# Attention by pairs of heads and blocks of queries in a two-block layer kernel

## The chip, the cores and the metric

The kernel runs on one core of a Trainium2 chip. The metric is the time of one launch on the device in microseconds; every figure of a run is that time, and the profiled execution also gives a span, from the first to the last instruction of the program.

## The reference

A sequence of 512 tokens of width 1024 goes through two layers, in float32. The first is a half feed-forward block (SwiGLU, 2816 wide), an attention block, a second half feed-forward block and a norm; the second is a mixing block (convolution and a recurrence) and a feed-forward block. The change lies in the attention block of the first. It has sixteen heads of two kinds, concatenated and projected:

```
# heads 0 to 7: own chunk of 64 and the 8 before it = all keys up to the chunk's end
sc = q_blk @ k.T * 64 ** -0.5 + bias[clip(i - j)]      # q, k, v: 512 x 64
# heads 8 to 15: q, k = 64 columns without and 32 with rotation, the same mask
sc = (q_nope @ k_nope.T + q_pe @ k_pe.T) * 96 ** -0.5
p = softmax(where(key_chunk <= query_chunk, sc, -1e30))
o = p @ v
x = x + concat(out_a, out_b) @ w_out
```

## The kernel before, in words

Activations lie feature by token in SBUF, 128 features to a tile. Weights come as 264 slabs of 128 x 1024, loaded by SyncE's queue into a ring of four (line 318). GpSimd splits each into a high and a low part (`split`, line 332: one pass with one input at line 335, one with two at line 337), and TensorE multiplies with three passes of products (lines 350 to 352). The engines run side by side and meet in semaphores; each works through its own list in order, so the order in which a function is called on an engine is part of the design.

Attention stands between the projections of the block (`in1`, `uq`, `ukv`) and its output projection (`out1`, line 664). It is cut into 64 steps: head h = 0 to 15, and for each head four blocks q of 128 queries, where block q sees L = 128 (q + 1) keys. Heads 2j and 2j+1 lie in the lower and the upper 64 partitions of the same tiles (`qa`, `ka`, or `qn`, `kn`). A step s is:

- TensorE, `scores` (line 597): for heads 0 to 7 one product with 64 rows; for the others one with 64 rows, one with 32 for the rotated part, and one with a single row that writes the mask, all added in one bank. Three banks alternate. In float32 each product is two records of weight load and product.
- VectorE, `score_max` (line 1578): the row maximum; for heads 0 to 7 it also adds the bias (from `relb`) and writes the sums to `prob`.
- ScalarE, `softmax` (line 1098): the exponential with its row sum into `prob`, which has three buffers.
- VectorE, `normalise` (line 1598): reciprocal and multiplication of `prob`.
- TensorE, `turn` (line 621): q + 1 transposes into one of two banks (3, 4).
- ScalarE, `keep_turned` (line 1110): the copy of the turned block to `probT`.

Once a head's four blocks are turned, `values` (line 630) does four products of 128 rows and 64 columns, over 512, 384, 256 and 128 queries, into bank 5 or 6, where the two heads of a pair fill the two column halves. Then `out_hi` on ScalarE (line 1119) and `out_lo` on VectorE (line 1605) split the pair's output for the projection.

TensorE runs one step of scores ahead, and turns two steps behind (lines 641 to 652). Between the steps of the first heads it also spreads the norms of the second kind of heads (`late_norm`, line 581, one in two steps up to s = 27): ten of them are 16 records in column halves (line 409) and one VectorE pass (line 1493), the last three are a product with a permutation (line 594) and three VectorE passes (lines 1572 to 1574). The first step of head 8 waits for these.

The bias table of a head comes by a transfer on ScalarE's queue (lines 1068 and 1132) into one of two buffers.

## Time and profile before

| | us |
|---|---|
| median of 3 runs (lowest, highest) | 1986.94 (1978.62, 1988.76) |
| the profiled execution, its own time | 1991.09 |
| its span | 1989.3 |
| granted clock, mean over the span | 0.931 |

The profiled execution is 4 us above the median. Times within a view count from the start of the span. The granted clock is TensorE's, as a share of 2.4 GHz; it has two levels, 1.0 and 0.5, and a number between them is a mean over a stretch. TensorE's products are pipelined: a record lasts longer than the time to the next one, so costs are read from start to start.

### The profile page before, as it was taken

What the parts mean: (1) busy time and instruction counts of PE and PEld (TensorE: products, weight loads), DVE (VectorE), ACT (ScalarE), POOL (GpSimd) and SP (SyncE); (2) the same over time, 40 slices, a digit from 0 to 9 for tenths busy, and PEclk for the clock granted to TensorE, in tenths of its full rate; (3) what the DMA queues carried; (4) which work ended last, traced back from release to release, by engine and by line L of the source; (5) the groups of instructions that cost most, each with busy time, mean ns of one, the idle gap of its engine ahead of it and who ended that gap; (6) DMA issues with size and microseconds to landing.
All of it is one profiled execution on the core that took longest, in us unless ns stands there. A gap on an engine that the chain in (4) does not pass through costs nothing.

```text
span 1989.3 us, 27420 instructions
## 1 busy us (share of the span) xinstructions
PE 1870.5 (94%) x10498; PEld 1469.6 (74%) x10498; DVE 1015.8 (51%) x1441; ACT 379.1 (19%) x656; POOL 950.5 (48%) x532
## 2 busy tenths in 40 slices
PE   6999999999999999999999999987768999999996
PEld 4888888878744447888888877774657788888885
DVE  6655543321563223665565256648694576767213
ACT  2000000100342221111110022222413133233100
POOL 4766667645300005566667755630000526666674
PEclk9999999999896659999999989997888979999998
DMA  4444433322100002344444322210000212222332
GB/s 162 145 150 148 143 131 103 106 84 75 59 27 0 1 0 85 124 142 150 149 137 138 106 85 85 85 44 2 1 2 2 85 46 100 97 95 95 106 103 99
DMA packets 48799, 173.89 MB, mean 87 GB/s; under 512 B 5424, under 2 KB 5808, under 8 KB 48464
## 3 DMA queue, kind: packets, MB, share of 16 engines
q1 hardware_dynamic: 39888, 143.10, 21.3%
q10 hardware_dynamic: 8832, 29.63, 4.4%
q8 instruction: 63, 1.03, 0.2%
q14 instruction: 16, 0.13, 0.0%
HBM read 170.61 MB, written 2.10 MB: 87 GB/s over the span
## 4 chain that ended last, share of the span: by engine, by line
PE 91%; DVE 6%; ACT 2%; issue 1%; DMA 0%; SPq 0%; DVEq 0%; ACTq 0%
PE banks L350 23%; PE banks L351 23%; PE banks L352 23%; PE banks L720 4%; PE banks L636 3%; PE banks L396 2%; DVE in_arena L1708 2%; PE banks L614 2%; PE banks L613 2%; PE banks L627 2%; PE banks L610 1%; PE banks L409 1%; DVE h_lo L1371 1%; PE banks L389 0%; DVE tmp L1328 0%
## 5 line engine op out<-in xcount | busy, mean ns | idle before, releaser
L335 POOL TENSOR_SCALAR w_hi<-w_raw 128x1024 fp32r<-128x1024 f32 x264 | 301.0, 1140 | 996.2 <-DMA w_raw<-in_slabs 995.9
L337 POOL TENSOR_TENSOR w_lo<-w_raw,w_hi 128x1024 fp32r<-128x1024 f32 x264 | 650.0, 2462 | 22.0
L350 PE MATMUL banks<-h_hi,w_hi 128*128 128x512 f32 x1464 | 580.1, 396 | 27.7 <-DVE h_lo L1371 21.8
L351 PE MATMUL banks<-h_lo,w_hi 128*128 128x512 f32 x1464 | 575.3, 393 | 0.0
L352 PE MATMUL banks<-h_hi,w_lo 128*128 128x512 f32 x1464 | 574.7, 393 | 0.0
L350 PEld LDWEIGHTS banks<-h_hi,w_hi 128*128 128x128 f32 x1464 | 278.3, 190 | 90.7 <-issue 26.3
L352 PEld LDWEIGHTS banks<-h_hi,w_lo 128*128 128x128 f32 x1464 | 278.3, 190 | 58.7
L351 PEld LDWEIGHTS banks<-h_lo,w_hi 128*128 128x128 f32 x1464 | 278.4, 190 | 58.1 <-issue 1.0
L350 PE MATMUL banks<-act_hi,w_hi 128*128 128x512 f32 x528 | 205.4, 389 | 0.0
L351 PE MATMUL banks<-act_lo,w_hi 128*128 128x512 f32 x528 | 205.4, 389 | 0.0
L352 PE MATMUL banks<-act_hi,w_lo 128*128 128x512 f32 x528 | 205.4, 389 | 0.0
L1412 DVE TENSOR_TENSOR act_lo<-tmp,act_hi 128x512 f32 x66 | 112.1, 1699 | 8.1
L351 PEld LDWEIGHTS banks<-act_lo,w_hi 128*128 128x128 f32 x528 | 99.1, 188 | 20.6
L350 PEld LDWEIGHTS banks<-act_hi,w_hi 128*128 128x128 f32 x528 | 99.1, 188 | 20.6
L352 PEld LDWEIGHTS banks<-act_hi,w_lo 128*128 128x128 f32 x528 | 99.1, 188 | 20.5
L1420 DVE TENSOR_TENSOR tmp<-banks,tmp 128x512 f32<-128x512 f32 x44 | 30.4, 692 | 162.4 <-PE banks L352 161.5
L1328 DVE TENSOR_TENSOR tmp<-tmp 128x512 f32<-128x512 f32 x36 | 52.8, 1467 | 103.5 <-PE banks L352 93.5
L1457 DVE SCALAR_TENSOR_TENSOR xT<-banks,xT 128x512 f32<-128x512 f32 x24 | 16.6, 691 | 170.8 <-PE banks L352 170.8
L1434 DVE CUSTOM_DVE_ANT_0 adaw<-adaw,silc 128x1024 f32<-128x1024 f32 x48 | 101.5, 2114 | 4.5 <-DMA adaw<-in_ada 4.2
L1051 ACT ACTIVATE tmp<-tmp 128x512 f32<-128x512 f32 x44 | 27.9, 634 | 338.6 <-DVE tmp L1420 338.5
L720 PE MATMUL banks<-in_arena 64*64 64x64 f32 (+1 forms) x1792 | 70.4, 245 | 18.8 <-DVE in_arena L1746 6.4
L720 PEld LDWEIGHTS banks<-in_arena 64*64 64x64 f32 x1792 | 66.7, 147 | 24.1 <-DVE in_arena L1746 10.6
(289 smaller groups left out, 1897.8 us busy)
## 6 DMA issues: line engine op xcount, KB each, us to landing
w_raw<-in_slabs SPq DMA_DIRECT2D x264, 512.0 KB, 3.3
adaw<-in_ada ACTq DMA_DIRECT2D x48, 512.0 KB, 3.3
xT<-in_x SPq DMA_DIRECT2D x2, 1024.0 KB, 7.3
relb<-in_relb ACTq DMA_DIRECT2D x8, 256.0 KB, 2.6
out_y<-xT SPq DMA_DIRECT2D x8, 256.0 KB, 2.0
block<-in_block ACTq DMA_DIRECT2D x1, 704.0 KB, 3.9
silc<-in_ada ACTq DMA_DIRECT2D x1, 512.0 KB, 3.3
tmp<-in_rope ACTq DMA_DIRECT2D x1, 512.0 KB, 3.3
```

The source lines that it names most:

```text
L335: nc.gpsimd.tensor_scalar(w_hi[:, r, :], w_raw[:, r, :], 1.0, 1.0, ALU.mult, ALU.mult).then_inc(S("w_hi"), 1)
L337: nc.gpsimd.tensor_tensor(w_lo[:, r, :], w_raw[:, r, :], w_hi[:, r, :], ALU.subtract).then_inc(S("w_split"), 1)
L350: mm(out, hi, rhs_hi, start=start, stop=False, skip_group_check=True)
L351: mm(out, hi, rhs_lo, start=False, stop=False, skip_group_check=True)
L352: return mm(out, lo, rhs_hi, start=False, stop=stop, skip_group_check=True)
L396: last = mm(out[:, width * t:width * t + width], square[:, P * t:P * t + P], mask, start=start and t == 0, stop=True, skip_group_check=True)
L613: mm(out[:, 0:L], qn[e64, j, qs], kn[e64, j, 0:L], start=True, stop=False, skip_group_check=True)
L636: last = mm(bank[5 + (h // 2) % 2][CH * (h % 2):CH * (h % 2) + CH, P * kt:T], v[:, kt, CH * (h % 8):CH * (h % 8) + CH], probT[:, NT * (h % ...
L720: last = mm(out, block_of(lhs, operands, e, g, c), r, start=opens and i == 0, stop=i == len(pairs) - 1, skip_group_check=True)
L1328: v.tensor_tensor(tmp[:, 4, :], tmp[:, 4, :], tmp[:, j % 2, :], ALU.add).then_inc(S("norm_acc"), 1)
L1412: v.tensor_tensor(actl_t[:, bass.ds(at * T, T)], t, hi, ALU.subtract).then_inc(S("act_lo"), 1)
L1434: v.tensor_tensor_reduce(out=adaw[:, u, :], in0=adaw[:, u, :], in1=silc, scale=1.0, scalar=0.0, op0=ALU.mult, op1=ALU.add, accum_out=mod_s ...
```

## The change

The 64 steps become 32, t = 4p + qb: a pair p of heads and a block qb of queries. In each step both heads' score products stand one behind the other, kind by kind, and write banks 0 and 1 or 2 and 3. Both heads' transposes go to banks 4 and 5, one for each head; ScalarE copies the first and VectorE the second into `probT`, which now holds two steps. The values products are made in every step, for 128 queries and the keys so far, the two heads alternating. VectorE makes one reciprocal for both heads; the multiplication moves to GpSimd, between the splits of the third and the fourth slab of the output projection. The maximum is negated once for both heads. A late norm is spread in each of steps 1 to 13. Values of the first group all go to bank 6, those of the second to 6 and 7. The bias tables have four buffers, `prob` six. One semaphore without a reader is dropped.

The new lines (lines removed from the functions shown above are not repeated; indentation is cut):

```diff
-rope, vb, relb = tmp[:, 0:2, :], slot("vb", 34, 4), slot("relb", 38, 2)
+rope, vb, relb = tmp[:, 0:2, :], slot("vb", 34, 4), slot("relb", 38, 4)
-probT = slot("probT", 23, 8)
-prob = slot("prob", 31, 3)
+probT = slot("probT", 23, 4)
+prob = slot("prob", 28, 6)
...
-row_max, row_nmax, row_sum = small_t[:, 188:192], small_t[:, 192:196], small_t[:, 196:200]
+row_max, row_nmax, row_sum = small_t[:, 238:246], small_t[:, 246:254], small_t[:, 188:196]
...
+def pair_step(t):
+    p, qb = divmod(t, NT)
+    return p, qb, P * (qb + 1)
+def of_step(columns, t):
+    return columns[:, 2 * (t % 4):2 * (t % 4) + 2]
+def values_bank(p):
+    return 6 if p < 4 or p % 2 else 7
...
+def normalise(t):
+    _, _, L = pair_step(t)
+    pool.wait_ge(S("row_recip"), t + 1)
+    for e in range(2):
+        p = prob[:, 2 * (t % 3) + e, 0:L]
+        nc.gpsimd.tensor_scalar(p, p, of_step(row_sum, t)[:, e:e + 1], None, ALU.mult).then_inc(S("probs_normed"), 1)
 for r in range(RING):
     split(r, r, 16)
+before = SLAB_AT["out1"] // RING
+with pool.Fori(1, before) as i:
+    for r in range(RING):
+        split(i * RING + r, r, i * 16 + 16)
+for n in range(before * RING, SLAB_AT["out1"] + 3):
+    split(n, n % RING, 16 * (n // RING + 1))
+for t in range(8 * NT):
+    normalise(t)
+for n in range(SLAB_AT["out1"] + 3, (before + 2) * RING):
+    split(n, n % RING, 16 * (n // RING + 1))
+with pool.Fori(before + 2, N_LOADS // RING) as i:
     for r in range(RING):
         split(i * RING + r, r, i * 16 + 16)
...
+def scores(t):
+    p, qb, L = pair_step(t)
+    out = [bank[2 * (t % 2) + e] for e in range(2)]
+    qs = slice(P * qb, P * qb + P)
+    if t == 0:
         pe.wait_ge(S("hd_applied"), 11)
         pe.wait_ge(S("in1_raw"), 30)
+    if t == 4 * NT:
         pe.wait_ge(S("roped"), 3)
+    if 2 <= t < 4 * NT + 2:
+        pe.wait_ge(S("row_nmax"), t - 1)
+    elif t >= 2:
+        pe.wait_ge(S("probs"), 2 * (t - 1))
+    if p < 4:
+        for e in range(2):
+            e64 = slice(CH * e, CH * e + CH)
+            mm(out[e][:, 0:L], qa[e64, p, qs], ka[e64, p, 0:L], start=True, stop=True).then_inc(S("scores"), 1)
         return
+    p -= 4
+    for e in range(2):
+        e64 = slice(CH * e, CH * e + CH)
+        mm(out[e][:, 0:L], qn[e64, p, qs], kn[e64, p, 0:L], start=True, stop=False, skip_group_check=True)
+    for e in range(2):
+        at = 32 * ((2 * p + e) % 4)
+        e32 = slice(at, at + 32)
+        mm(out[e][:, 0:L], qr[e32, p // 2, qs], kr[e32, 0, 0:L], start=False, stop=False,
+           skip_group_check=True, tile_position=(at, 0))
+    for e in range(2):
+        at = 32 * ((2 * p + e) % 4)
+        e1 = slice(at, at + 1)
+        mm(out[e][:, L - CH:L], const("maskq")[e1, :], const("maskk")[e1, :], start=False, stop=True,
+           skip_group_check=True, tile_position=(at, 0)).then_inc(S("scores"), 1)
+def turn(t):
+    _, qb, _ = pair_step(t)
+    for e in range(2):
+        pe.wait_ge(S("probs_normed"), 2 * t + e + 1)
+        if t >= 1:
+            pe.wait_ge(S(f"probT{e}"), t)
+        for kt in range(qb + 1):
+            last = nc.tensor.transpose(bank[4 + e][:, P * kt:P * kt + P], prob[:, 2 * (t % 3) + e, P * kt:P * kt + P], ident)
+        last.then_inc(S(f"turned{e}"), 1)
+def values(t):
+    p, qb, _ = pair_step(t)
+    v = va if p < 4 else vb
+    if qb == 0 and p >= 1 and p != 4:
+        pe.wait_ge(S("o_lo"), p if p < 4 else p - 1)
+    for e in range(2):
+        pe.wait_ge(S(f"probT{e}"), t + 1)
+    for kt in range(qb + 1):
+        for e in range(2):
+            h = 2 * (p % 4) + e
+            last = mm(bank[values_bank(p)][CH * e:CH * e + CH, P * qb:P * qb + P], v[:, kt, CH * h:CH * h + CH],
+                      probT[:, 2 * (t % 2) + e, P * kt:P * kt + P], start=qb == 0 and kt == 0, stop=kt == qb,
+                      skip_group_check=True)
     last.then_inc(S("values"), 1)
 scores(0)
+for i in range(8 * NT + 2):
+    if i + 1 < 8 * NT:
+        scores(i + 1)
+    if 1 <= i <= 13:
+        late_norm(i - 1)
+    if 1 <= i <= 8 * NT:
+        turn(i - 1)
+    if i >= 2:
+        values(i - 2)
-pe.wait_ge(S("probT"), 16 * NT)
...
-for h in range(2):
+for h in range(4):
+    act.dma_start(relb[:, h, :], relb_in[h]).then_inc(S(f"relb_in{h // 2}"), 16)
 raw = {"cq0": cq[:, 0, :], "cq1": cq[:, 1, :], "ckv0": ckv[:, 0, :], "kr0": kr[:, 0, :]}
 for j in range(4):
...
+def softmax(t):
+    p, _, L = pair_step(t)
+    act.wait_ge(S("row_nmax"), t + 1)
+    if t >= 4:
+        act.wait_ge(S("probs_normed"), 2 * (t - 3))
+    for e in range(2):
+        if p >= 4:
+            act.wait_ge(S(f"turned{e}"), t - 2)
+        dst = prob[:, 2 * (t % 3) + e, 0:L]
+        src = dst if p < 4 else bank[2 * (t % 2) + e][:, 0:L]
+        f(dst, src, ACT.Exp, bias=of_step(row_nmax, t)[:, e:e + 1],
+          accum_out=of_step(row_sum, t)[:, e:e + 1]).then_inc(S("probs"), 1)
+def keep_turned(t):
+    _, _, L = pair_step(t)
+    act.wait_ge(S("turned0"), t + 1)
+    if t >= 2:
+        act.wait_ge(S("values"), t - 1)
+    f(probT[:, 2 * (t % 2), 0:L], bank[4][:, 0:L], ACT.Copy).then_inc(S("probT0"), 1)
 def out_hi(p):
+    act.wait_ge(S("values"), NT * p + NT)
+    f(h_hi[:, p, :], bank[values_bank(p)][:, :], ACT.Copy).then_inc(S("o_hi"), 1)
+for i in range(8 * NT + 3):
+    if i < 8 * NT:
+        softmax(i)
+        p, qb, _ = pair_step(i)
+        if qb == 3 and p < 2:
+            for e in range(2):
+                b = 2 * p + e
+                act.dma_start(relb[:, b, :], relb_in[4 + b]).then_inc(S(f"relb_in{p}"), 16)
+    if 2 <= i < 8 * NT + 2:
+        keep_turned(i - 2)
+    if i >= 3 and (i - 3) % NT == 3:
+        out_hi((i - 3) // NT)
 norm_squares("ffn2", xT, lambda j: act.wait_ge(S("x_new"), 8 + j + 1))
...
+def score_max(t):
+    p, _, L = pair_step(t)
+    for e in range(2):
+        s = bank[2 * (t % 2) + e][:, 0:L]
+        dve.wait_ge(S("scores"), 2 * t + e + 1)
+        if p >= 4:
+            last = v.tensor_reduce(of_step(row_nmax, t)[:, e:e + 1], s, AXX, ALU.max, negate=True)
+            continue
+        b = 2 * (p % 2) + e
+        if t % NT == 0:
+            dve.wait_ge(S(f"relb_in{p % 2}"), 32 * (p // 2 + 1))
+        if t >= 3:
+            dve.wait_ge(S(f"turned{e}"), t - 2)
+        last = v.tensor_tensor_reduce(out=prob[:, 2 * (t % 3) + e, 0:L], in0=s, in1=relb[:, b, T - L:T], scale=1.0,
+                                      scalar=LOWEST, op0=ALU.add, op1=ALU.max,
+                                      accum_out=of_step(row_max, t)[:, e:e + 1])
+    if p < 4:
+        link(last)
+        last = v.tensor_scalar(of_step(row_nmax, t), of_step(row_max, t), -1.0, None, ALU.mult)
+    last.then_inc(S("row_nmax"), 1)
+def row_recip(t):
+    dve.wait_ge(S("probs"), 2 * t + 2)
+    v.reciprocal(of_step(row_sum, t), of_step(row_sum, t)).then_inc(S("row_recip"), 1)
+def keep_turned(t):
+    _, _, L = pair_step(t)
+    dve.wait_ge(S("turned1"), t + 1)
+    if t >= 2:
+        dve.wait_ge(S("values"), t - 1)
+    v.tensor_copy(probT[:, 2 * (t % 2) + 1, 0:L], bank[5][:, 0:L]).then_inc(S("probT1"), 1)
 def out_lo(p):
     dve.wait_ge(S("o_hi"), p + 1)
+    v.tensor_tensor(h_lo[:, p, :], bank[values_bank(p)][:, :], h_hi[:, p, :], ALU.subtract).then_inc(S("o_lo"), 1)
+for i in range(8 * NT + 3):
+    if i < 8 * NT:
+        score_max(i)
+    if 1 <= i <= 8 * NT:
+        row_recip(i - 1)
+    if 2 <= i < 8 * NT + 2:
+        keep_turned(i - 2)
+    if 1 <= i <= 13:
+        late_norm(i - 1)
+    if i >= 3 and (i - 3) % NT == 3:
+        out_lo((i - 3) // NT)
 add_half(8, SLAB_AT["out1"], 1, 1.0, "ffn2")
```

## Rows read from the trace of the kernel before

**Rows 1.** The page: span, TensorE's busy time, the chain that ended last by engine.
```profile
span 1989.3 us, 27420 instructions
PE 1870.5 (94%) x10498; PEld 1469.6 (74%) x10498; DVE 1015.8 (51%) x1441; ACT 379.1 (19%) x656; POOL 950.5 (48%) x532
...
PE 91%; DVE 6%; ACT 2%; issue 1%; DMA 0%; SPq 0%; DVEq 0%; ACTq 0%
```

**Rows 2.** Busy time in attention's two stretches, whose ends are attention's.
```profile
core 0: us, PE busy (x) PEld busy (x) DVE busy (x) ACT busy (x) POOL busy (x), PEclk, DMA share, GB/s
528.70:600.00 71.30, 68.31 (x382) 35.67 (x383) 47.43 (x174) 30.39 (x91) 3.40 (x2) 0.90 0.10 33
600.00:745.40 145.40, 144.47 (x361) 69.80 (x361) 35.57 (x110) 36.18 (x108) 0.00 (x0) 0.60 0.00 0
```

**Rows 3.** The same view around one burst of values products in the second group.
```profile
617.20:620.60 3.40, 3.40 (x7) 1.34 (x6) 0.23 (x1) 0.52 (x2) 0.00 (x0) 0.50 0.00 0
620.60:624.00 3.40, 3.40 (x20) 2.33 (x18) 1.11 (x4) 0.73 (x3) 0.00 (x0) 0.99 0.02 5
624.00:634.30 10.30, 10.30 (x21) 4.54 (x20) 3.37 (x10) 3.39 (x9) 0.00 (x0) 0.50 0.00 0
```

**Rows 4.** TensorE in order of time, second group: start us, us, instruction, count.
```profile
605.27 0.70 PE L613 MATMUL banks<-kn,qn 64*128 64x256 f32 x2
...
606.69 0.66 PE L627 MATMUL banks<-both,prob 128*128 128x128 f32 x3
...
611.79 2.07 PE L613 MATMUL banks<-kn,qn 64*128 64x512 f32 x2
...
616.11 0.47 PE L627 MATMUL banks<-both,prob 128*128 128x128 f32 x1
616.52 4.39 PE L636 MATMUL banks<-probT,va 128*64 128x512 f32 x8
```

**Rows 5.** The same view, first group, at the upper clock.
```profile
575.05 0.91 PE L610 MATMUL banks<-ka,qa 64*128 64x384 f32 x2
575.89 0.66 PE L627 MATMUL banks<-both,prob 128*128 128x128 f32 x4
576.48 1.09 PE L409 MATMUL banks<-both,small 128*64 128x128 f32 x16
577.50 1.12 PE L610 MATMUL banks<-ka,qa 64*128 64x512 f32 x2
578.55 0.33 PE L627 MATMUL banks<-both,prob 128*128 128x128 f32 x1
```

**Rows 6.** The same view, line 754: two products in two row halves, then one.
```profile
1226.27 1.13 PE L754 MATMUL banks<-in_arena 64*128 64x512 f32 x4
...
1230.28 1.12 PE L754 MATMUL banks<-in_arena 64*128 64x512 f32 x2
```

**Rows 7.** Groups by line in attention, VectorE and ScalarE: count, busy us, mean ns, idle before.
```profile
L1116 ACT ACTIVATE probT<-banks 128x128 f32<-128x128 f32 (+1 forms) x64 | 27.5, 431 | 110.9 <-PE banks L627 110.9
L1107 ACT ACTIVATE prob<-prob,small 128x128 f32<-128x128 f32 (+3 forms) x32 | 18.0, 561 | 37.1 <-DVE small L1593 37.0
L1107 ACT ACTIVATE prob<-banks,small 128x128 f32<-128x128 f32 (+3 forms) x32 | 16.8, 524 | 0.4
L1595 DVE TENSOR_REDUCE small<-banks 128x1 f32<-128x128 f32 (+3 forms) x32 | 15.7, 492 | 98.7 <-PE banks L618 98.7
L1590 DVE CUSTOM_DVE_ANT_0 prob<-banks,relb 128x128 f32<-128x128 f32 (+3 forms) x32 | 15.5, 486 | 0.5 <-PE banks L627 0.4
L1107 ACT ACTIVATION_READ_ACCUMULATOR prob<-banks,small 128x1 f32 x32 | 6.4, 201 | 0.0
L1493 DVE SCALAR_TENSOR_TENSOR qn<-qn,small,banks 128x512 f32<-128x512 f32 x4 | 3.0, 748 | 7.9 <-PE banks L409 7.9
```

**Rows 8.** The same view, GpSimd: its last two passes before attention's end.
```profile
L337 POOL TENSOR_TENSOR w_lo<-w_raw,w_hi 128x1024 fp32r<-128x1024 f32 x1 | 2.4, 2352 | 0.1
L335 POOL TENSOR_SCALAR w_hi<-w_raw 128x1024 fp32r<-128x1024 f32 x1 | 1.0, 1047 | 9.3 <-DMA w_raw<-in_slabs 9.3
```

More of the change, by code:

```diff
@@ L621, in turn @@
-            def turn(s):
-                pe.wait_ge(S("probs_normed"), s + 1)
-                if s >= 2:
-                    pe.wait_ge(S("probT"), s - 1)
-                for kt in range(s % NT + 1):
-                    last = nc.tensor.transpose(bank[3 + s % 2][:, P * kt:P * kt + P], prob[:, s % 3, P * kt:P * kt + P], ident)
-                last.then_inc(S("turned"), 1)
-            def values(h):
-                pe.wait_ge(S("probT"), NT * h + NT)
-                if h % 2 == 0 and h >= 4:
-                    pe.wait_ge(S("o_lo"), h // 2 - 1)
-                v = va if h < 8 else vb
-                for kt in range(NT):
-                    last = mm(bank[5 + (h // 2) % 2][CH * (h % 2):CH * (h % 2) + CH, P * kt:T],
-                              v[:, kt, CH * (h % 8):CH * (h % 8) + CH], probT[:, NT * (h % 2) + kt, P * kt:T],
-                              start=kt == 0, stop=kt == NT - 1, skip_group_check=True)
+                if 2 <= t < 4 * NT + 2:
+                    pe.wait_ge(S("row_nmax"), t - 1)
+                elif t >= 2:
+                    pe.wait_ge(S("probs"), 2 * (t - 1))
@@ L639, in values @@
                 last.then_inc(S("values"), 1)
             scores(0)
-            for s in range(16 * NT + 2):
-                if s + 1 < 16 * NT:
-                    scores(s + 1)
-                if s >= 2:
-                    turn(s - 2)
-                    if s % 2 and s <= 27:
-                        late_norm((s - 3) // 2)
-                    if (s - 2) % NT == 0 and s > 2:
-                        values((s - 2) // NT - 1)
-            values(15)
+            for i in range(8 * NT + 2):
[7 more added lines that the diff above has]
+                    values(i - 2)
@@ L1449, in gains_made @@
                 v.tensor_tensor(gp["mixpost"], mod[:, 16:24], vec("mix_post_g", 0, 8), ALU.mult)
-                v.tensor_tensor(gp["ffnpost"], mod[:, 40:48], vec("ffn_post_g", 0, 8), ALU.mult).then_inc(S("mod_ready"), 1)
+                v.tensor_tensor(gp["ffnpost"], mod[:, 40:48], vec("ffn_post_g", 0, 8), ALU.mult)
             def add_half(o, at, n_slabs, scale, norm):
```

90 lines of the change are left out of this document (removed).

## Prediction

> **What bounds the kernel now.** I read the page first, then the busy time by stretch, then TensorE's instructions in order of time in both groups of heads, then the groups of instructions by line. On the page the reader is to see that TensorE is busy 94% of the span and makes 91% of the chain that ended last [rows 1]: the kernel is its TensorE stream, one stage after another, so a microsecond that TensorE saves in a stage is a microsecond of the end. The change touches one stage, attention, from 528.8 us to 745.4 us, 216.6 us. Its stretches [rows 2] are unlike: the first group of heads takes 71 us (granted clock 0.90), the second 145 us with TensorE busy for 144 of them at a mean clock of 0.60, while VectorE and ScalarE work a quarter of it. So the second group is bound by TensorE, and mostly at the lower of its two levels (1.2 GHz against 2.4). The order in time shows what goes with the level [rows 3, 4]: during a burst of values products (all 128 rows, eight records) the clock is still 0.50, right behind it 0.99, and when the score products return, which use 64, then 32 rows, then one, it is at half again until the next burst. At the upper level a whole score step of 256 keys takes 605.27 to 606.69, 1.42 us; at the lower one of 512 keys takes 611.79 to 616.11, 4.32 us.
>
> **The sum, part by part.** I work per step of the new schedule: one pair of heads, one block of 128 queries, 128 to 512 keys. There are 16 steps in each group (64 single-head steps become 32).
>
> *Both heads' scores adjacent.* The two heads lie in different halves of the rows and write different banks. The trace has exactly such a pair elsewhere: two 64-row products of 512 columns into two banks, four records, in 1.13 us, where one alone, two records, takes 1.12 us [rows 6]. So I charge a pair what one head costs now. First group, upper level: 1.05 us for 512 keys (577.50 to 578.55) and 0.84 us for 384 (575.05 to 575.89) [rows 5], so 0.21 us per 128 keys above 0.2 us of entry: 0.42, 0.63, 0.84, 1.05, mean 0.73. Second group: 1.42 us for 256 keys [rows 4] is twice 0.43 for the two products plus 0.56 for the mask and entries, so 0.99, 1.41, 1.84, 2.27, mean 1.63. If rows did not overlap, each would be some 0.5 and 1.3 us more.
>
> *Values per block.* Today eight records of both passes of 512 to 128 columns. Then two heads' products of 128 columns alternate between column halves; the norm products do that now, 16 records in about 1.02 us (576.48 to 577.50) [rows 5], 0.13 us for a product, so 0.26 to 1.02 us a step, mean 0.64, where one head now takes 4.39 us at half clock for its four blocks in one burst [rows 4]. More weight loads are issued, which those rows already contain.
>
> *Transposes* are unchanged: four take 0.59 us (575.89 to 576.48) [rows 5]: 0.107 each, a single pass of 128 columns by the slope above, and 0.16 of entry, so two heads' worth is 0.37 to 1.02, mean 0.70. TensorE's own work is then 0.73 + 0.64 + 0.70 = 2.1 us a step in the first group, 3.1 with the 1.02 us of late norm that 10 steps carry, and 1.63 + 0.64 + 0.70 = 3.0 in the second.
>
> *The other engines* [rows 7]. VectorE loses the multiplications and takes over half of the turned copies, ScalarE loses those; both were idle for most of the stretch. The exponentials and maxima stay. GpSimd gets 64 multiplications of 128 to 512 columns. The nearest row is its own one-input pass over 1024 columns, 1047 ns [rows 8]. Below, scaled by width to the mean of 320 columns, it is 0.33 us; above, if width gave nothing back, 1.05; the dearest row of that engine, 2352 ns for two inputs, is the far end. I take 0.45, near the width scaling as the operation is the same, with a little fixed cost. The weight splits before it are finished by about 536 us and one slab waits behind the 64; it is needed three slabs after attention, so this costs nothing as long as GpSimd is done with attention before TensorE is. The bias tables are loaded earlier than before, and the dropped semaphore has no reader in time: nothing for both.
>
> *The new waits.* The turned banks are no longer alternated, one for each head. So the transposes of a step wait for both copies of the step before, and ScalarE's copy is queued behind the exponentials of the following step. This makes a ring over two steps: maxima (2 x 0.49), exponentials (2 x (0.52 + 0.20)), copy 0.43, transposes 0.70, values 0.64, scores 1.63, and five handoffs of some 0.08 us that I estimate from the gaps between rows: 6.2 us for two steps, 3.1 a step. Widths are uneven, and the ring through the steps of 256 and 512 keys is the longer: over four steps values and scores 5.2 in place of 4.5, transposes 1.2 in place of 1.4, and maxima, exponentials and copies of 384 keys on average in place of 320, by the same rows some 0.6 more. That is 13.5 us per four steps, **3.4 a step**, above TensorE's 3.0. Second group: 16 x 3.4 = 54 us. In the first group the ring is maxima 1.39 (with the negation), exponentials 1.50, copy 0.43, transposes 0.70, values 0.64, scores 0.73, handoffs 0.6, and the late norm in it, 1.02 on TensorE and 0.75 on VectorE: 7.8 for two, 4.0 a step with uneven widths. Thirteen steps make 52, the three rope steps (three passes of 0.69 in place of one of 0.75) 2, three free steps at 3.1 make 9, the fill 2: 65 us. At the end the last chain drains unhidden, 4 us. All at the upper level: 65 + 54 + 4 = 123 us.
>
> *The clock.* I do not expect all of it at 2.4 GHz. Both facts of [rows 3] speak for the change: score products now use both halves of the rows at once, and full-row values come in every step in place of every fourth. Against it stands that TensorE gets holes (3.0 of 3.4 us). At the lower level the same second-group step is TensorE-bound: 4.32 us for 512 keys and their like, averaging 2.8, and twice 1.3 for the rest, 5.5 us. With four of 16 steps there the second group is 12 x 3.4 + 4 x 5.5 = 63, and the first group starts low as it does now, 3 us more. **65 + 3 + 63 + 4 = 135 us, against 216.6: 82 less.** From the profiled execution's own 1991.1 us that is 1909; the median of the runs is 4 us lower, **1905 us**. Nothing behind attention is anchored in time, so all of it should arrive.
>
> *Two rules of the skill.* On GpSimd the trace has 1047 ns for one input and 2352 ns for two at equal width [rows 8]. The Trainium skill, GPSIMD Engine Reference, section 4.1, prefers VectorE for elementwise work, GpSimd being about twice slower for two inputs and roughly line-rate for one; by its line-rate clause the sum is as above, by the factor of two the multiplication would be 0.8 us, still inside the bounds. On the copies out of PSUM the rows give 431 ns on average, one engine each [rows 7]. The Trainium skill, TensorEngine Tiling, section PSUM Bottleneck, warns that packing speeds up the products and not the evacuation; that is the ring above, and if packing gave nothing past it the sum would stay at 3.4 a step.
>
> **The rivals.** (a) *The clock stays at half through the second group*, since holes and 32-row and one-row products remain. For: it is at 0.60 today with TensorE hardly ever idle [rows 2]. Against: [rows 3]. Then 65 + 5 + 16 x 5.5 + 3 = 161, 56 less: 1931. (b) *GpSimd is dear*, 2.35 us for each multiplication. It sits in front of every transpose, two per step, behind the maxima of the next step: 0.98 + 0.15 + 4.7 + 0.35 + 0.64 + 1.63 + 0.4 = 8.9 for two steps, but GpSimd itself needs 4.7 a step. So 16 x 4.7 + 13 x 5.1 + 3 x 4.7 + 6 = 162: 1932. (c) *The row halves do not overlap here*: 16 x 0.5 + 16 x 1.3 = 29 more than my sum: 1934. Against: [rows 6]. (d) *Slower than before.* The in-order queues serialise the steps: a step's maxima, exponentials, reciprocal, normalising, transposes, copy, values and scores, 0.98 + 1.45 + 0.15 + 0.9 + 0.70 + 0.43 + 0.64 + 1.63 + 0.6 = 7.5 us, run without the next one beside them. Its place is the wait of the transposes on GpSimd; it decides once the mean step passes 216.6 / 32 = 6.8 us. Then 32 x 7.5 = 240: 2010. Against: scores are issued one step ahead and three pairs of buffers exist. (e) *All at the upper level and no more than the rings*: 123 us, 94 less: 1893.
>
> **How the numbers follow.** Forecast with (e) as its fast end 0.56, (a) 0.25, (b) or something between on the handoffs 0.13, (c) 0.04, (d) 0.02. The range goes from a little under (e) to beyond (a) to (c): 1886 to 1945, leaving out (d), part of (b) with (a), and a ring that is shorter than I think. Half a per cent is about 10 us, what a measurement of this kernel can tell from no change. Only (d) is slower; 0.01 for an unforeseen stop that ends within 10 us. Faster 0.97, same 0.01, slower 0.02.
>
> **What would show it.** Right: the second group's stretch some 60 us long, clock above 0.85, score records of the two heads a few ns apart, an idle TensorE released by the turned copies, GpSimd rows of 0.3 to 0.6 us. Wrong: a clock near 0.6 with TensorE busy throughout (a); transposes waiting for GpSimd (b); score records one behind the other (c); a step of over 6.8 us (d).

## The result and the profile after

The changed kernel took **1903.9 us** (median of 4 runs, 1902.4 to 1905.3) beside 1984.7 us before (1978.6 to 1988.8): a ratio of 0.960, 95% interval 0.957 to 0.962. The forecast was 1905 us. The profiled execution took 1903.4 us with a span of 1901.5 us, 87.8 us shorter than before. The page (answers to [rows 1]):

```profile
span 1901.5 us, 27741 instructions
PE 1769.7 (93%) x10690; PEld 1438.3 (76%) x10690; DVE 998.4 (53%) x1361; ACT 363.8 (19%) x624; POOL 1016.6 (53%) x596
...
PE 88%; DVE 7%; issue 2%; ACT 2%; POOL 1%; DMA 0%; SPq 0%; DVEq 0%; ACTq 0%
```

TensorE does 100.8 us less, and GpSimd appears in the chain. Attention, from its first score product to the first product of the projection behind it, took 135.7 us in place of 216.6, so 80.9 of the 87.8 us came from there. The busy time by stretch (answers to [rows 2]), cut at the last exponentials of steps 15 and 31, and one pair of heads of the second group:

```profile
core 0: us, PE busy (x) PEld busy (x) DVE busy (x) ACT busy (x) POOL busy (x), PEclk, DMA share, GB/s
529.00:588.30 59.30, 49.48 (x458) 29.87 (x458) 38.31 (x132) 23.12 (x76) 29.07 (x28) 0.93 0.09 31
588.30:654.80 66.50, 60.67 (x430) 38.83 (x428) 25.54 (x70) 25.29 (x85) 34.17 (x32) 0.80 0.00 1
654.80:664.70 9.90, 6.96 (x50) 5.32 (x50) 1.75 (x5) 2.78 (x7) 8.90 (x6) 0.69 0.01 2
...
620.60:637.70 17.10, 15.58 (x112) 9.97 (x110) 6.40 (x19) 6.32 (x22) 8.54 (x8) 0.80 0.00 1
```

The second group's clock rose from 0.60 to 0.80, and its steps take 17.1 us for four. TensorE in order of time there (answers to [rows 4, 6]; last in brackets the idle time before and what released it):

```profile
620.13 0.49 PE L650 MATMUL banks<-kn,qn 64*128 64x128 f32 x4
620.55 0.49 PE L654 MATMUL banks<-kr,qr 32*128 32x128 f32 x4
620.88 0.34 PE L659 MATMUL banks<-block 1*128 1x64 f32 x4
622.46 0.52 PE L670 MATMUL banks<-both,prob 128*128 128x128 f32 x3 [1.25 <-ACT probT L1164]
623.25 0.55 PE L670 MATMUL banks<-both,prob 128*128 128x128 f32 x3 [0.27 <-POOL prob L358]
623.72 0.66 PE L684 MATMUL banks<-probT,vb 128*64 128x128 f32 x8
624.31 1.08 PE L650 MATMUL banks<-kn,qn 64*128 64x256 f32 x4
```

Four score records, two heads, stand in one group: both heads share the time of one. The hole of 1.25 us comes once for each pair of heads and ends with ScalarE's copy of turned rows; a little more waits for GpSimd. Behind it the score products of 256 keys take 1.08 us, the lower level (0.70 at the upper). GpSimd by form (answers to [rows 8]: count, busy us, mean ns, idle before):

```profile
L358 POOL TENSOR_SCALAR prob<-prob,small 128x512 f32<-128x512 f32 x16 | 24.8, 1563 | 1.2 <-DVE small L1649 1.1
L358 POOL TENSOR_SCALAR prob<-prob,small 128x384 f32<-128x384 f32 x16 | 19.7, 1242 | 17.1 <-DVE small L1649 17.1
L358 POOL TENSOR_SCALAR prob<-prob,small 128x256 f32<-128x256 f32 x16 | 14.6, 922 | 27.2 <-DVE small L1649 27.2
L358 POOL TENSOR_SCALAR prob<-prob,small 128x128 f32<-128x128 f32 x16 | 9.8, 626 | 22.7 <-DVE small L1649 22.7
...
L349 POOL TENSOR_SCALAR w_hi<-w_raw 128x1024 fp32r<-128x1024 f32 x1 | 1.0, 1044 | 0.0
```

A multiplication took 1.09 us on average, not 0.45. So the total was right while one term was off by more than a factor of two, and the second group was not at full clock. Two of the prediction's own signs of being right did not come: the second group's clock is 0.80 where I asked for more than 0.85, and the GpSimd rows are 0.63 to 1.56 us where I asked for 0.3 to 0.6. The experiments ask three things: what the dear multiplication costs, what the rest of the ring costs, and on what the clock hangs.

### The profile page after: what moved, and what is told of

Its sections match the earlier page's. It is cut to its first block, busy times and chain, and to the rows that moved or that the text cites. A ratio compares the mean times of both kernels' runs of the same rounds, so it can differ in the third digit from the quotient of the medians.

```text
span 1901.5 us, 27741 instructions
## 1 busy us (share of the span) xinstructions
PE 1769.7 (93%) x10690; PEld 1438.3 (76%) x10690; DVE 998.4 (53%) x1361; ACT 363.8 (19%) x624; POOL 1016.6 (53%) x596
## 3 DMA queue, kind: packets, MB, share of 16 engines
q8 instruction: 64, 1.05, 0.2%
## 4 chain that ended last, share of the span: by engine, by line
PE 88%; DVE 7%; issue 2%; ACT 2%; POOL 1%; DMA 0%; SPq 0%; DVEq 0%; ACTq 0%
PE banks L381 24%; PE banks L383 24%; PE banks L382 24%; PE banks L765 4%; PE banks L427 3%; DVE in_arena L1761 2%; PE banks L684 1%; POOL prob L358 1%; PE banks L670 1%; PE banks L440 1%; PE banks L650 1%; PE banks L654 1%; DVE h_lo L1417 1%; PE banks L420 1%; DVE tmp L1374 0%
## 5 line engine op out<-in xcount | busy, mean ns | idle before, releaser
L1458 DVE TENSOR_TENSOR act_lo<-tmp,act_hi 128x512 f32 x66 | 121.3, 1838 | 8.1
L1503 DVE SCALAR_TENSOR_TENSOR xT<-banks,xT 128x512 f32<-128x512 f32 x24 | 16.6, 691 | 170.9 <-PE banks L383 170.9
L358 POOL TENSOR_SCALAR prob<-prob,small 128x128 f32<-128x128 f32 (+3 forms) x64 | 68.8, 1089 | 68.3 <-DVE small L1649 68.1
L1480 DVE CUSTOM_DVE_ANT_0 adaw<-adaw,silc 128x1024 f32<-128x1024 f32 x48 | 86.8, 1808 | 4.4 <-DMA adaw<-in_ada 4.1
```

The costliest lines, as they stand in the source:

```text
L358: nc.gpsimd.tensor_scalar(p, p, of_step(row_sum, t)[:, e:e + 1], None, ALU.mult).then_inc(S("probs_normed"), 1)
L1458: v.tensor_tensor(actl_t[:, bass.ds(at * T, T)], t, hi, ALU.subtract).then_inc(S("act_lo"), 1)
L1480: v.tensor_tensor_reduce(out=adaw[:, u, :], in0=adaw[:, u, :], in1=silc, scale=1.0, scalar=0.0, op0=ALU.mult, op1=ALU.add, accum_out=mod_s ...
```

## The experiments

The kernels ran in three sets, each on one chip beside the kernel before, whose median was 1987.0, 1973.0 and 1976.1 us; times are compared inside a set. The changed kernel itself ran again only in the third set, so in the first two a version is set against it by attention in the profile and by the ratio to before (0.960 above, 0.965 in the third set; a difference of a few thousandths is within the noise). Each profile shows one execution. My theory (G and R): the wait on GpSimd and the ring through ScalarE's copy make the longer step. The rivals: the clock's falls do it, whatever fills the time between (C, later H: TensorE's holes bring those falls), or the mix of products does (M). "Pair" is the time from the exponentials of 512 keys of one pair of heads to those of the next.

### First set: the multiplication, and the adjacency of the scores

**Normalising back on VectorE**, behind the reciprocal; nothing on GpSimd.

```diff
-                v.reciprocal(of_step(row_sum, t), of_step(row_sum, t)).then_inc(S("row_recip"), 1)
+                link(v.reciprocal(of_step(row_sum, t), of_step(row_sum, t)))
+                L = pair_step(t)[2]
+                for e in range(2):
+                    p = prob[:, 2 * (t % 3) + e, 0:L]
+                    v.tensor_scalar(p, p, of_step(row_sum, t)[:, e:e + 1], None, ALU.mult).then_inc(S("probs_normed"), 1)
```

> Both multiplications of a step go back to VectorE, right behind the reciprocal; all else is the changed kernel. In the kernel before, VectorE takes 0.29 to 0.49 us for one (128 to 512 columns), in the changed kernel GpSimd takes 0.63 to 1.56 us, so a step's pair costs 0.77 us instead of 2.18 on average. Theory G (GpSimd's multiplication in front of the transposes is what makes a step of the second group 4.27 us where I had 3.4): the second group falls from about 70 to 54 to 60 us, the first by up to 10, and the time is 1880 to 1892. Rival C (the clock's falls make the longer step, whatever fills the holes): 1900 to 1906, with the clock of the stretch still near 0.83. Rival Q (VectorE's in-order queue then holds maxima, multiplications, late norm and half of the copies, and the first group, where VectorE is busy for 40 of 65 us, gets longer): first group 5 us longer or more, second shorter, 1890 to 1905.

Measured: 1896.1 us, ratio 0.957 (0.954 to 0.960); attention 126.4 us. The second and the third of the four pairs of the second group:

```profile
605.20:618.60 13.40, 12.15 (x110) 7.94 (x110) 8.83 (x25) 6.27 (x21) 0.00 (x0) 1.00 0.01 1
618.60:632.10 13.50, 12.25 (x112) 8.04 (x110) 8.93 (x26) 6.35 (x22) 0.00 (x0) 1.00 0.01 2
```

13.45 us for four steps is 3.36 a step: this is the 3.4 of my ring, at the upper level. TensorE's one hole is still 1.25 us and still ends with ScalarE's copy:

```profile
618.89 0.34 PE L656 MATMUL banks<-block 1*128 1x64 f32 x4
620.48 0.84 PE L667 MATMUL banks<-both,prob 128*128 128x128 f32 x6 [1.25 <-ACT probT L1161]
```

The pair at the group's entry took 18.0 us at a clock of 0.68, and that keeps the gain at 9 us of attention. Theory G had the second group right (58.3 us, 54 to 60 expected), but the first group gained nothing (59.4 us) and the time missed its range by 4 us. Q (first group 5 us longer) did not come.

**Head 0 on VectorE, head 1 on GpSimd, at the same time.**

```diff
+                dve.wait_ge(S("row_recip"), 2 * t + 1)
+                p = prob[:, 2 * (t % 3), 0:pair_step(t)[2]]
+                v.tensor_scalar(p, p, of_step(row_sum, t)[:, 0:1], None, ALU.mult).then_inc(S("row_recip"), 1)
...
-                for e in range(2):
+                for e in (1,):
                     p = prob[:, 2 * (t % 3) + e, 0:L]
```

> Head 0 of each pair is normalised by VectorE behind the reciprocal, head 1 by GpSimd at the same time. The later of the two is ready 1.09 us after the reciprocal on average (1.56 for 512 columns), where the changed kernel needs 2.18 (3.11). Theory G: most of the gain of the version with everything on VectorE, with only half of its load on VectorE's queue: 1885 to 1895. Rival C (clock alone): 1900 to 1906. Rival P (GpSimd and VectorE slow each other down when both work in place on float32 rows in SBUF): rows of either multiplication longer than 0.49 and 1.56 us at 512 columns.

Measured: 1895.7 us, 0.955 (0.953 to 0.958); attention 121.9 us (in the fastest of the four runs). The last two pairs are again 13.4 to 13.5 us at 1.00; the two before them are 17.1 us at 0.71 and 16.6 us at 0.79. The second and the third pair:

```profile
598.90:615.50 16.60, 15.35 (x112) 10.17 (x110) 7.90 (x23) 6.31 (x22) 5.10 (x4) 0.79 0.00 1
615.50:628.90 13.40, 12.15 (x111) 7.94 (x109) 7.71 (x22) 6.29 (x21) 5.10 (x4) 1.00 0.01 2
```

Both hold the same single hole of TensorE, 1.25 us, ended by ScalarE's copy. In the first of them the clock falls behind the hole and in the second it does not, so a hole of this length can go with a fall but does not settle it.

P holds for one side: VectorE's rows keep 286 to 486 ns, GpSimd's grow.

```profile
L358 POOL TENSOR_SCALAR prob<-prob,small 128x512 f32<-128x512 f32 x8 | 14.8, 1856 | 5.3 <-DVE small L1650 4.7
L358 POOL TENSOR_SCALAR prob<-prob,small 128x128 f32<-128x128 f32 x8 | 5.6, 694 | 27.2 <-DVE small L1650 27.2
```

**Constants in place of the per-row scalar on GpSimd.**

```diff
-  nc.gpsimd.tensor_scalar(p, p, of_step(row_sum, t)[:, e:e + 1], None, ALU.mult).then_inc(S("probs_normed"), 1)
+  nc.gpsimd.tensor_scalar(p, p, 1.0, 1.0, ALU.mult, ALU.mult).then_inc(S("probs_normed"), 1)
```

> GpSimd multiplies by the constants 1.0 and 1.0 in place of the per-row reciprocal, so the normalising is left out; every wait and every instruction count stays. The slab conversion, which has that form, takes 1.05 us for 1024 columns, that is about 1 ns a column; the normalising takes 2.4 ns a column above 0.31 us. If the per-row scalar is what makes it dear, the rows are 0.4 to 0.8 us (0.45 was my term), and by theory G the time is 1880 to 1895. If the float32 output or the work in place makes it dear, the rows stay at 0.63 to 1.56 us and the time at 1900 to 1907.

This kernel leaves the normalising out. Measured: 1895.2 us, 0.956 (0.953 to 0.959); attention 121.5 us. Its two stretches and the drain, cut as in the changed kernel, then two forms of the multiplication:

```profile
528.90:583.60 54.70, 44.79 (x464) 28.55 (x464) 38.71 (x132) 23.16 (x77) 11.86 (x28) 1.00 0.10 32
583.60:644.20 60.60, 54.80 (x424) 36.01 (x422) 25.48 (x69) 25.24 (x85) 14.05 (x32) 0.86 0.00 1
644.20:650.40 6.20, 4.29 (x51) 3.43 (x51) 1.75 (x5) 2.79 (x7) 5.40 (x6) 1.00 0.00 0
```

```profile
L358 POOL TENSOR_SCALAR prob<-prob 128x512 f32<-128x512 f32 x16 | 9.6, 617 | 8.8 <-DVE small L1649 8.8
L358 POOL TENSOR_SCALAR prob<-prob 128x128 f32<-128x128 f32 x16 | 4.5, 297 | 32.4 <-DVE small L1649 32.4
```

The four widths average 457 ns. Engine, tensor, width, place and output type are the same; the kernel makes two multiplications by constants in place of one by the row's scalar, and still the pass is shorter. So the per-row scalar is what makes it 2.1 to 2.5 times as long. My 0.45 us was the price of the other form. The dear form costs 14.2 us of attention beside this one: 4.6 in the first group, 5.9 in the second, 3.7 in the drain, waits and clock together.

**Scores head by head in the second group.**

```diff
                     mm(out[e][:, 0:L], qn[e64, p, qs], kn[e64, p, 0:L], start=True, stop=False, skip_group_check=True)
-                for e in range(2):
                     at = 32 * ((2 * p + e) % 4)
...
                        skip_group_check=True, tile_position=(at, 0))
-                for e in range(2):
-                    at = 32 * ((2 * p + e) % 4)
                     e1 = slice(at, at + 1)
```

> In the second group the four score products of a pair go head by head (64 rows, 32 rows, mask; then the same of the other head) instead of product by product with both heads adjacent. If the row halves overlap because they are adjacent, as the records of the changed kernel a few ns apart say, a step's two wide products cost about 0.35 us more each at 320 columns at the upper level, 0.8 to 1.3 us a step at the clock's mean, so 13 to 21 us if TensorE bounds the second group, and 5 to 13 if the holes (17% of it) take part of it: 1909 to 1925. The clock would also tell: if single row halves pull it down, the second group's clock falls from 0.83 toward 0.6 and the time passes 1930. Rival: adjacency does nothing, the products of different rows overlap in any order: 1901 to 1906.

Measured: **1968.4 us**, 0.990 (0.987 to 0.994); attention 202.2 us. The whole second group, then one pair of it, then its records of 512 keys:

```profile
581.70:727.00 145.30, 144.20 (x484) 85.49 (x482) 30.05 (x78) 28.51 (x91) 42.53 (x38) 0.51 0.00 1
615.20:649.70 34.50, 34.50 (x110) 20.24 (x108) 6.93 (x19) 6.44 (x22) 8.57 (x8) 0.50 0.00 0
```
```profile
640.19 2.07 PE L650 MATMUL banks<-kn,qn 64*128 64x512 f32 x2
642.19 2.07 PE L653 MATMUL banks<-kr,qr 32*128 32x512 f32 x2
644.06 0.52 PE L656 MATMUL banks<-block 1*128 1x64 f32 x2
644.51 2.07 PE L650 MATMUL banks<-kn,qn 64*128 64x512 f32 x2
```

This is the kernel before again, 145 us for the group [rows 2], though values and transposes come in every step and GpSimd works as in the changed kernel. Of the change's 80.9 us of attention, 66.5 hang on the order of these products. A pair takes 34.5 us at 0.50 against 17.1 at 0.80. The second branch of my expectation came (clock toward half, past 1930), and both effects are in it. TensorE's work in a pair with the overlap is 12.15 us at the upper level (first version above), by my estimate 24.3 at the lower: the overlap takes 34.5 to 24.3, the level and the holes 24.3 to the 17.1 of the changed kernel, and 12.15 would be left at the upper level without holes. The overlap by itself was priced about right (24.3 to 34.5 is 10.2 us a pair, 5.1 at the upper level, 1.3 a step); the loss of the clock with it was not in my rival (c).

### Second set: values, and ScalarE's order

**Values head by head**, both groups.

```diff
-                for kt in range(qb + 1):
-                    for e in range(2):
+                for e in range(2):
+                    for kt in range(qb + 1):
```

> Values products go head by head (all blocks of head 0 into the lower column half, then all of head 1) in both groups, instead of alternating between the halves. In the changed kernel 16 records of alternating products take 1.09 us, 0.136 us a product; a product of two passes of 128 columns alone takes 0.21 us by the transposes' slope. So a step's values grow by 0.4 us on average, 13 us over 32 steps at the upper level where TensorE bounds, 6 to 10 where holes take part of it: 1910 to 1920. Head by head the scores cost 64 us because the granted clock of the whole second group went to 0.50. If the values' half use of the columns does the same, 1960 or more; if the clock looks at rows and not at columns, it stays near 0.8 and the first figure holds. Rival: values of different halves overlap in any order: 1901 to 1906.

Measured: 1913.8 us (2 runs), 0.969 (0.964 to 0.975); attention 142.8 us, 7.1 more than in the changed kernel. Pairs 17.8 to 19.1 us, two of them:

```profile
605.30:623.10 17.80, 16.28 (x111) 10.87 (x110) 6.42 (x19) 6.34 (x22) 8.56 (x8) 0.81 0.00 1
623.10:642.20 19.10, 17.61 (x110) 11.51 (x110) 6.32 (x18) 6.26 (x21) 8.56 (x8) 0.73 0.00 1
```

As expected. Sixteen records of values take 1.58 us in place of 1.09, and the second group's clock is 0.70 to 0.81: it did not collapse, as it did when the scores went head by head.

**The copy of turned rows ahead of the exponentials on ScalarE**, then the same with normalising on VectorE, then with it split.

```diff
             for i in range(8 * NT + 3):
+                if 2 <= i < 8 * NT + 2:
+                    keep_turned(i - 2)
                 if i < 8 * NT:
                     softmax(i)
...
-                if 2 <= i < 8 * NT + 2:
-                    keep_turned(i - 2)
```

> The changed kernel with one order turned round on ScalarE: the copy of the turned rows of step i-2 goes ahead of the exponentials of step i, not behind them. GpSimd keeps its dear multiplications. Theory R (the ring: at the upper level TensorE's one hole for each pair of heads, 1.25 us, is a transposition waiting for ScalarE's copy queued behind exponentials): this hole goes. In the changed kernel that leaves the hole at GpSimd, so TensorE still stops once per pair; if any such stop costs the clock as it does now, the pair stays near 17.1 us and the time is 1896 to 1903; if the clock now holds, 13 to 14 us a pair and 1885 to 1895. Rival: the exponentials come later by the copy and the maxima behind them wait, no gain: 1902 to 1908.

> The version with all multiplications on VectorE, and ScalarE's copy ahead of the exponentials. With VectorE alone the last three pairs took 13.45 us each at clock 1.00 with TensorE busy for 12.2 of them and one hole of 1.25 us behind the exponentials of 512 keys. Theory R: the hole goes, a pair takes 12.2 to 12.6 us, the one low-clock pair may not occur: attention 116 to 123 us in place of 126, time 1884 to 1892. Rival: VectorE's queue (8.9 us of work in 13.4) makes the next hole, and the pair stays at 13.4: 1893 to 1898.

> Head 0 normalised on VectorE and head 1 on GpSimd, and ScalarE's copy ahead of the exponentials. Attention took 121.9 us with the split alone, two of the second group's pairs at a clock of 0.71 and 0.79 (17 us) and the rest at 1.00 (13.4). Theory R: 12.2 to 12.8 us a pair at the upper level, attention 112 to 118: 1882 to 1890, the fastest of all. Rival (the holes that cost the clock are those at the rope steps, before the second group): the two low pairs stay and only 2 to 3 us come: 1890 to 1894.

Measured: 1900.8 us, 0.964 (0.959 to 0.969); 1884.2, 0.954 (0.950 to 0.959); 1887.9, 0.956 (0.952 to 0.961). Attention 132.7, 115.0 and 113.0 us (the last in the fastest of its four runs, 1879.9 us). The first gained 3 us of attention and nothing in the time that can be told from noise; the third has the shortest attention but not, as I expected, the shortest time. Pairs of the first, and one of the second, which has no GpSimd in it:

```profile
618.10:632.20 14.10, 12.61 (x112) 7.97 (x110) 6.40 (x19) 6.54 (x22) 8.54 (x8) 1.00 0.00 1
632.20:649.20 17.00, 15.13 (x105) 9.74 (x104) 6.35 (x19) 6.50 (x21) 8.54 (x8) 0.80 0.01 1
```
```profile
583.40:599.70 16.30, 16.27 (x108) 10.61 (x106) 8.93 (x26) 6.54 (x22) 0.00 (x0) 0.71 0.00 0
599.70:612.20 12.50, 12.29 (x110) 7.91 (x109) 8.73 (x26) 6.40 (x21) 0.00 (x0) 1.00 0.00 1
```

Theory R holds: with cheap multiplications the pair fell from 13.45 to 12.5 us and TensorE is busy for 12.29 of them. With GpSimd's dear ones a pair of the same kernel runs in 14.1 us at 1.00 or in 17.0 at 0.80. So the multiplication's direct cost is 14.1 less 12.5, 1.6 us a pair in this order, and the clock's is 2.9. Both pairs of the first kernel have the same two holes, 0.82 and 0.67 us, both ended by GpSimd, and one kept the upper level: as in the split version, the holes alone do not say which.

### Third set: holes and the clock

**Unneeded products in TensorE's hole**, in the changed kernel as it stands.

```diff
+                if i >= 4 * NT and i % NT == 3:
+                    pe.wait_ge(S("o_lo"), i // NT)
+                    for _ in range(2):
+                        mm(bank[13 - values_bank(i // NT)], qn[:, 0, 0:P], kn[:, 0, :], start=True, stop=True)
                 if 1 <= i <= 8 * NT:
                     turn(i - 1)
```

> The changed kernel plus work that it does not need: in each pair of the second group, ahead of the transposes of the 384-key step, where TensorE stands still for some 2.3 us because GpSimd is not done, two products of 128 rows and 512 columns (1.05 us each at the upper level) go into the values bank that is free; nothing reads them. Theory H (it is TensorE's hole that costs the clock afterwards, not the longer handoff itself): the clock of a pair goes from 0.80 to 1.00 and the pair from 17.1 to 14.2 to 15 us although TensorE does more; attention 124 to 130 us in place of 135.7, time 1892 to 1900. Rival M (the mix of the score products sets the clock, holes do not matter): the clock stays at 0.80, the pair gets 0 to 3 us longer, 1904 to 1916.

> The changed kernel once more, beside the others of this call: 0.957 to 0.962 of the kernel before; pairs of the second group 17.1 us at a clock of 0.80. If the pattern of the clock is one of several that this kernel falls into by chance, pairs at 14 to 15 us at 1.00 appear in it as well.

Measured: **1892.7 us** with the extra work (6 runs, 1891.0 to 1899.7), **1901.8** without (6 runs, 1900.6 to 1902.5) on the same chip; ratios to before 0.961 (0.955 to 0.967) and 0.965 (0.959 to 0.971). Attention 125.0 against 135.2 us. One pair of each, the filled kernel first:

```profile
615.50:629.60 14.10, 14.10 (x116) 8.74 (x114) 6.40 (x20) 6.30 (x21) 8.54 (x8) 1.00 0.01 1
```
```profile
619.10:636.20 17.10, 15.58 (x110) 9.94 (x110) 6.38 (x19) 6.32 (x22) 8.56 (x8) 0.80 0.00 1
```

TensorE does 2.0 us more a pair (16 records at a busy time of 7.9 us in four pairs) and the pair is 3.0 us shorter, with GpSimd's work untouched. The stand-still itself cost little, the lower level that went with it did. H holds against M as M was put: with the same score products and none added, pairs run at 1.00 in the versions with cheap multiplications and in two pairs of the first copy-first version, so the mix of the scores alone does not hold the clock at 0.80. But the added products use all 128 rows, so this run does not tell a filled hole from more full-row work. And H in its plain form, one hole and one fall, is not shown: with holes of 1.25 us or 0.82 + 0.67 us left open, pairs ran at either level. Where the holes were filled or cut to 0.2 us (here, and with the copy first and VectorE), the last three pairs all ran at 1.00. One number of my expectation was off: the hole is 1.25 + 0.27 us in most pairs, 2.26 only in the last. The repeated kernel fell into the same pattern, pair for pair (17.1, 17.1, 17.1), so the pattern is not drawn anew in each run.

**Only the 32-row products and masks head by head.**

```diff
                     mm(out[e][:, 0:L], qr[e32, p // 2, qs], kr[e32, 0, 0:L], start=False, stop=False,
                        skip_group_check=True, tile_position=(at, 0))
-                for e in range(2):
-                    at = 32 * ((2 * p + e) % 4)
                     e1 = slice(at, at + 1)
```

> In the second group only the 32-row products and the masks go head by head; the 64-row products of both heads stay adjacent. At the upper level a 32-row product costs up to 0.35 us more a step at 320 columns, its entries some 0.2: 6 to 9 us over 16 steps. Head by head in both kinds cost 64 us, of which the overlap explains 13 to 21 and the clock (0.50 throughout) the rest. If the clock needs the wide products to be paired and not the narrow ones, it stays near 0.8 here: 1908 to 1920. If 32-row products one at a time are enough to hold it at half, the second group's clock is 0.5 to 0.65 and the time 1935 to 1960.

Measured: 1902.1 us, 0.965 (0.957 to 0.973), pairs 17.1 us at 0.80. The edit did not take the 32-row products apart:

```profile
633.48 1.13 PE L650 MATMUL banks<-kn,qn 64*128 64x512 f32 x4
634.54 1.13 PE L654 MATMUL banks<-kr,qr 32*128 32x512 f32 x4
635.50 0.34 PE L657 MATMUL banks<-block 1*128 1x64 f32 x4
```

The second head's 32-row product still overlaps the first's. The first head's mask product stands between them in the program, but its record starts behind both (635.50). So this run says nothing on whether narrow products alone would hold the clock down; that is open.

**Two unneeded products at the entry of the second group**, on the version with VectorE and the copy first.

```diff
+                if i == 14:
+                    pe.wait_ge(S("roped"), 3)
+                    mm(bank[7], qn[:, 0, 0:P], kn[:, 0, :], start=True, stop=True)
                 if 1 <= i <= 8 * NT:
                     turn(i - 1)
+                if i == 14:
+                    mm(bank[7], qn[:, 0, 0:P], kn[:, 0, :], start=True, stop=True)
```

> The version with all multiplications on VectorE and the copy first, plus two unneeded products of 128 rows and 512 columns at the step before the second group begins, one in each of TensorE's two holes there (1.31 and 1.13 us). In that version the pair after these holes is the only one of the second group at a low clock (0.71, 16.3 us; the others 12.5 us at 1.00). Theory H: that pair takes 12.5 to 13.5 us too, 3 us less: 1880 to 1883. Rival: the clock falls for what lies earlier (the three rope steps), the pair stays at 16 us or more and the time at 1884 to 1888.

Measured: **1882.3 us** (6 runs, 1875.2 to 1885.9), 0.955 (0.949 to 0.961); attention 111.7 us in place of 115.0.

```profile
581.20:593.80 12.60, 11.90 (x104) 7.49 (x102) 8.89 (x27) 6.49 (x21) 0.00 (x0) 1.00 0.00 0
593.80:606.40 12.60, 12.39 (x112) 8.02 (x110) 8.82 (x26) 6.46 (x22) 0.00 (x0) 1.00 0.01 1
```

The pair that took 16.3 us at 0.71 takes 12.6 at 1.00, as Theory H said; here too the added products are full-row work as well as filling. Beside the changed kernel on the same chip this version is 19.5 us (1.0%) faster, and the ranges do not touch. Its 3.3 us over the version without the two products are seen in the profile; the two ratios to before (0.955 and 0.954) are too coarse for them: the kernel before itself ran from 1951.4 to 1981.3 us in this set.

## Why the prediction was right, point by point

- **The scores of a pair cost what one head's do**: right. 512 keys take 1.13 us for both heads (the x4 rows of the 32-row experiment), as the neighbouring stage had shown [rows 6], and the 32-row products likewise. Undone, it cost 66.5 us of attention.
- **Values per block**: right. 16 records in 1.09 us; the pair's whole TensorE work at the upper level is 12.15 us, 3.04 a step, where I had 3.0.
- **The ring through the turned copies, 3.4 a step**: right at the upper level, 3.36 with the multiplications cheap, the hole ends with ScalarE's copy, and turning ScalarE's order round took the hole away. My sum had GpSimd outside this ring; with its multiplications at 0.46 us (constants) the pair was 13.4 us, so that held.
- **GpSimd's multiplication, 0.45 us**: the step that failed. It measured 1.09 on average and 1.56 at 512 columns, above my upper bound of 1.05, because the row I scaled [rows 8] multiplies by constants and this one by a scalar for each row. "The operation is the same" was the false reading: the operand was not. Direct cost in the second group where the clock holds: at most the 0.65 us a pair between 13.45 and the filled kernel's 14.1, and that pair is full of TensorE work (12.15 and the added 2.0), so the multiplication's own share of it is not shown. With the clock it cost 14.2 us of attention.
- **The clock, 4 of 16 steps at half**: a little short. 0.80 in a pair of 17.1 us is 6.8 us at the lower level, which at my 5.5 us a step is 1.2 steps of four, 5 of 16. The cause I named (holes) is borne out so far, that filling or closing them brought the upper level; but what a fall hangs on is not shown: 13.45 us with a hole of 1.25 runs at 1.00, 17.1 us with 1.25 + 0.27 at 0.80, and equal holes ran at either level in the split version. My step at the lower level was also a little short: by the rows of the kernel before, 384 keys take 3.47 us (607.28 to 610.75) and 512 take 4.32, which makes the mean 3.0 and not 2.8, the step 5.7 and four of them 1 us more. Second group by the forecast 63 us, measured 66.5.
- **First group and drain**: 65 + 3 us forecast, 59.3 measured to the exponentials of step 15; its transposes and values come after that mark, so part of the 8.7 us belongs to what follows. The drain was 9.9 us where I had 4, with 3.1 us of GpSimd for its last two multiplications and a clock of 0.69. Sum 135.7 against 135: the slack of the first group took up the dear drain and the slower steps.
- **The luck in the number**: the kernel with constants has the multiplication that I had priced (0.46 us), and its attention took 54.7 + 60.6 + 6.2 = 121.5 us against my 68 + 63 + 4 = 135. So with my own price the sum was 13.5 us too long, by these marks nearly all of it in the first group, and the dear multiplication put 14.2 us back. The pairing was right as a mechanism; 1905 came out of two errors of opposite sign. A smaller pair stands beside it: I took 4 us off the profiled execution for the median, which the changed kernel did not show (1903.9 beside 1903.4), and 6.9 us came outside attention.
- **All of it arrives behind attention**: right. The span lost 6.9 us more than attention did. They came in the recurrence, where the same 826 TensorE records took 84.6 us at 0.76 before and 77.4 at 0.86 after. Outside attention the thirteen profiles of the changed kernel and its relatives show 1763 to 1770 us and the kernel before 1773, and no part of the change was aimed at it. Where the recurrence's holes fall against the clock is the likely reason; no run tests it, and why the kernel before drew the worse pattern is open.
- **The rivals**: (a), half clock throughout, is what the scores head by head bring, so its place was real and the pairing is what kept it away; of the two facts of [rows 3] that I put against it, the full-row values alone (they were in every step there) did not lift the clock, the paired scores did. (b) was half right in its premise (dear, at 1.09 and not 2.35), and the wait was in front of the transposes where I put it. (c) put 29 us on lost overlap at the upper level and missed that the clock goes with it. (d) never came near: 4.2 us a step against 6.8. (e), 123 us as the fast end, is not the floor: with the copies first, attention took 111.7 to 115.0 us.

```profile
1351.70:1436.30 84.60, 64.23 (x826) 43.24 (x824) 60.31 (x100) 33.85 (x54) 0.00 (x0) 0.76 0.01 2
```
```profile
1271.10:1348.50 77.40, 57.13 (x826) 41.34 (x824) 60.29 (x100) 33.85 (x54) 0.00 (x0) 0.86 0.01 1
```

The two fences are the recurrence in the kernel before and then after, in the view of [rows 2].

## What to carry to other kernels

Issue products that use different row groups next to each other: here it halved the score work and also kept TensorE's clock up, and of the 17.4 us a pair that it was worth some 10 go to the overlap and 7 to the clock (an estimate; taken in the other order the clock has the larger part). Before moving an elementwise pass to GpSimd find a row with the same kind of scalar operand, and put the in-order queue's short work that TensorE waits for (copies out of the turned banks) ahead of the long work of the next step. Where TensorE has one short hole in each round and a granted clock below one, try to fill the hole or close it, and judge by the clock of that round and not by the hole's length: here equal holes ran at either level.

## What the runs showed of the hardware that I had not expected

- **More work, less time.** 2.0 us of unneeded full-row products a pair made the pair 3.0 us shorter, with the granted clock at 1.00 in place of 0.80. The Trainium skill, TensorE: Matmul & The Clock Gate, Part 1, says that the level follows how busy TensorE has been of late; this run agrees. By that alone the kernel with its scores head by head, busy for 34.50 of 34.50 us, should have had the upper level, and it had 0.50: busy time in the records does not tell the level by itself. The same products side by side had 0.80 to 1.00.
- **A per-row scalar on GpSimd** costs 626 to 1563 ns for 128 to 512 columns, constants 297 to 617 ns, where VectorE's per-row form takes 0.29 to 0.49 us.
- **GpSimd beside VectorE**: with a VectorE multiplication of 286 to 486 ns started at the same time, GpSimd's grew by 68 ns (128 columns) to 293 ns (512), and VectorE's did not. The Trainium skill, SBUF — State Buffer, section Who interferes with whom, says of the ports that the two engines share that whoever issues first holds them for its whole instruction and the other is blocked; the growth here was less than VectorE's instruction, a quarter of it to six tenths. Whether VectorE's multiplication used those ports, no run here shows.
- **Overlap past a product of other rows**: a 32-row product ran beside its neighbour's although a one-row mask product stood between them in the program (the mask's record starts 0.95 us behind both). With a 32-row product and a mask between two 64-row products there was none.
